# The grouped norm of the scan in four column strips, with its factor spread by one-row products

## What is computed

```
u = y.reshape(b, L, SSD_INNER) * jax.nn.silu(z.astype(f32))
ug = u.reshape(b, L, SSD_GROUPS, SSD_INNER // SSD_GROUPS)
ug = ug * lax.rsqrt(jnp.mean(ug * ug, axis=-1, keepdims=True) + EPS)
u = (ug.reshape(b, L, SSD_INNER) * norm_w.astype(f32)).astype(h.dtype)
y_ssd = u @ w_ssd_out
```

## Time and profile before

| | |
|---|---|
| median of 3 runs | 1366.25 us (1364.44 to 1367.7) |
| the profiled execution, its own time | 1368.92 us |
| its span in the profile | 1367.2 us |
| TensorE busy | 1214.0 us, 89% of the span |
| VectorE busy | 552.6 us, 40% |
| ScalarE busy | 389.2 us, 28% |
| GpSimd busy | 462.5 us, 34% |
| TensorE's share of the chain that ended last | 61% |
| mean granted clock of TensorE | 0.963 of full speed |

### The profile page before, as it was taken

How to read it: one execution, slowest core, us unless ns; L and a number is a source line. 1 busy time by engine, 2 the same in 40 slices (tenths; PEclk the granted TensorE clock), 3 DMA queues, 4 the chain that set the end, 5 groups by cost and what they waited for, 6 DMA issues and landing times.

```text
span 1367.2 us, 22226 instructions
## 1 busy us (share of the span) xinstructions
PE 1214.0 (89%) x8633; PEld 1038.6 (76%) x8633; DVE 552.6 (40%) x823; ACT 389.2 (28%) x572; POOL 462.5 (34%) x358
## 2 busy tenths in 40 slices
PE   4999999999998999989989999999996978877771
PEld 4999999999876976887687679999995645443440
DVE  5445532003654955585576563014443241021112
ACT  4122124343324433342343362222324101010112
POOL 5444432333533444263345354344220111111100
PEclk7999999999999999999999999999997999999996
DMA  6232222324203510540252123343639899999974
GB/s 151 64 91 77 77 62 62 83 76 126 70 17 102 139 47 1 159 108 20 73 152 63 31 87 89 83 126 103 226 122 383 322 396 401 403 398 383 393 254 148
DMA packets 185571, 210.75 MB, mean 154 GB/s; under 512 B 12166, under 2 KB 161798, under 8 KB 176754
## 3 DMA queue, kind: packets, MB, share of 16 engines
q1 hardware_dynamic: 176626, 193.41, 42.6%
q0 software_dynamic: 5040, 9.72, 2.8%
q10 hardware_dynamic: 3822, 6.39, 1.2%
HBM read 191.56 MB, written 26.57 MB: 160 GB/s over the span
## 4 chain that ended last, share of the span: by engine, by line
PE 61%; DVE 11%; DMA 9%; SPq 9%; issue 5%; ACT 4%; DVEq 1%; ACTq 0%; POOLq 0%
PE acc L627 37%; SPq L549 8%; DVE area L1202 4%; PE acc L890 4%; PE pTS L1010 3%; DMA area<-in_w_down 2%; PE pTS L739 2%; DMA area<-in_w_up 2%; PE acc L1040 2%; DMA ring<-in_w_in 2%; DMA ring<-in_w_up 2%; PE pTS L797 1%; PE pY L791 1%; PE pY L815 1%; DVE big L1264 1%
## 5 line engine op out<-in xcount | busy, mean ns | idle before, releaser
L627 PE MATMUL acc<-h_parts,ring_parts 128*128 128x328 f32 (+1 forms) x3840 | 546.9, 303 | 21.7 <-issue 7.0
L627 PEld LDWEIGHTS acc<-h_parts,ring_parts 128*128 128x128 f32 x3840 | 532.6, 190 | 38.1 <-issue 37.9
L1858 POOL TENSOR_TENSOR ring_parts<-ring,ring_parts 128x1024 fp32r<-128x1024 f32 x112 | 283.0, 2527 | 461.4 <-ACT ring_parts L1566 461.4
L1566 ACT ACTIVATE ring_parts<-ring 128x1024 fp32r<-128x1024 f32 x112 | 118.4, 1058 | 414.1 <-PE acc L627 366.9
L1010 PE MATMUL pTS<-area,big 128*64 128x256 f32 x672 | 109.1, 404 | 17.0 <-DMA area<-in_w_gate 7.2
L627 PE MATMUL acc<-u_parts,ring_parts 128*128 128x264 f32 (+1 forms) x640 | 109.4, 299 | 0.0
L1010 PEld LDWEIGHTS pTS<-area,big 128*64 128x64 f32 x672 | 66.5, 145 | 50.2 <-DMA area<-in_w_gate 10.8
L627 PEld LDWEIGHTS acc<-u_parts,ring_parts 128*128 128x128 f32 x640 | 96.4, 188 | 0.0
L1202 DVE SCALAR_TENSOR_TENSOR area<-area,xvec 128x616 f32<-128x616 f32 x72 | 90.1, 1252 | 10.5 <-DVE area L1200 0.6
L627 PE MATMUL acc<-area_parts,ring_parts 128*128 128x264 f32 (+1 forms) x512 | 91.1, 299 | 0.0
L627 PEld LDWEIGHTS acc<-area_parts,ring_parts 128*128 128x128 f32 x512 | 78.4, 188 | 0.0
(11 more groups left out here) (349 smaller groups left out, 1523.8 us busy)
## 6 DMA issues: line engine op xcount, KB each, us to landing
ring<-in_w_in SPq DMA_DIRECT2D x80, 512.0 KB, 3.9
area<-in_w_gate SPq DMA_DIRECT2D x21, 1024.0 KB, 17.6
area<-in_w_up SPq DMA_DIRECT2D x21, 1024.0 KB, 18.8
area<-in_w_down SPq DMA_DIRECT2D x21, 1024.0 KB, 23.9
area<-in_state_ssm SPq DMA_DIRECT2D x16, 512.0 KB, 6.8
out<-area SPq DMA_DIRECT2D x16, 512.0 KB, 6.7
ring<-in_w_ssd_out SPq DMA_DIRECT2D x16, 512.0 KB, 4.0
ring<-in_w_gate SPq DMA_DIRECT2D x7, 1024.0 KB, 24.0
```

What stands on the lines that cost most here:

```text
L627: m = nc.tensor.matmul(acc[a][:, h, 0:n], w[s][:, k, :], x[:, k, h * HALF:h * HALF + n], start=first and k == 0 and w is w_hi and x is hi, ...
L1566: a_.activation(w_hi[b % 2], w_raw[b % 2], ACT.Copy).then_inc(hi_done, 1)
L1858: gp.tensor_tensor(w_lo[b % 2], w_raw[b % 2], w_hi[b % 2].bitcast(F32), ALU.subtract).then_inc(lo_done, 1)
```

## The change

A constant `QT` = 148, a quarter of the tokens, is new.

1. The sums: for each of the four depth steps four products of 32 columns of ones by 148 tokens. Strip j of the array takes tokens 148 j onward and writes partitions 32 j to 32 j + 31 of `pT`. So each quarter's sum stands on 32 partitions, at the same columns.
2. The root and the reciprocal are one instruction each, on all 128 partitions and 148 columns.
3. TensorE then spreads the reciprocal: for each quarter a product of one row of ones (row 32 j) by one row of `rms`, into `pT` (quarters 0, 1) and `pS` (2, 3). The order is 0, 2, 1, 3, with a wait for the first two before the third, as quarters of one bank come from different rows of the array.
4. VectorE multiplies u by the factor from PSUM, in 8 instructions of 296 columns in place of 4 of 592.
5. TensorE: block 11 moves from the start of the next turn to before the jump, its first half ahead of the sums, its second half behind them, then the wait for `s_rm` and the spreading. So the loop's turn begins with block 2. Block 1 of the first group moves ahead of the loop, and the gate blocks after it begin with 2.
6. The wait for `s_rm` before the transposes becomes one for `s_un`; counts of semaphores follow.

```diff
             pe.wait_ge(s_dta, 7)
-            pe_block(pe, g_block(0, 0), 0, hT_hi, hT_lo)
+            for b in range(2):
+                pe_block(pe, g_block(0, b), b, hT_hi, hT_lo)
             with pe.Fori(0, GROUPS) as g:
-                for b in range(1, 7):
+                for b in range(2, 7):
                     pe_block(pe, g_block(g, b), b, hT_hi, hT_lo)
                 pe_block(pe, g_block(g, 7), 7, hT_hi, hT_lo, part=0)
                 pe.wait_ge(s_silu, g * 6 + 8)
-                pe.wait_ge(s_rm, g + 1)
+                pe.wait_ge(s_un, g + 1)
...
+                pe_block(pe, g_block(g, 11), 11, hT_hi, hT_lo, part=0)
                 pe.wait_ge(s_so, g + 1)
                 pe.wait_ge(s_sq, g + 1)
-                for h, pb in ((0, pT), (1, pS)):
-                    n = HALF if h == 0 else T - HALF
-                    for k in range(GK):
-                        m = nc.tensor.matmul(pb[:, 0:n], ones[:, :], sq[:, k, h * HALF:h * HALF + n],
+                for k in range(GK):
+                    for j in range(4):
+                        m = nc.tensor.matmul(pT[32 * j:32 * j + 32, 0:QT], ones[:, 0:32], sq[:, k, j * QT:(j + 1) * QT],
                                              start=k == 0, stop=k == GK - 1)
                 m.then_inc(p_gn, 1)
-
-            for n in range(1, 4):
+                pe_block(pe, g_block(g, 11), 11, hT_hi, hT_lo, part=1)
+                pe.wait_ge(s_rm, g * 2 + 2)
+                for j in (0, 2, 1, 3):
+                    if j == 1:
+                        pe.wait_ge(p_gn, g * 5 + 3)
+                    nc.tensor.matmul((pT, pS)[j // 2][:, j % 2 * QT:(j % 2 + 1) * QT], ones[32 * j:32 * j + 1, :],
+                                     rms[32 * j:32 * j + 1, :], start=True, stop=True).then_inc(p_gn, 1)
+
+            for n in range(2, 4):
...
-                dve.wait_ge(s_rm, g + 2)
+                dve.wait_ge(s_rm, g * 2 + 1)
                 link(v.reciprocal(rms, rms))
+                dve.sem_inc(s_rm, 1)
+                dve.wait_ge(p_gn, g * 5 + 5)
                 for k in range(GK):
                     u_k = uT[:, bass.ds(g * GK + k, 1), :].rearrange("p a b -> p (a b)")
-                    x = v.scalar_tensor_tensor(u_k, u_k, dg[:, k, 1:2], rms, ALU.mult, ALU.mult)
+                    for q, pb in ((0, pT), (1, pS)):
+                        u_q = u_k[:, q * 2 * QT:(q + 1) * 2 * QT]
+                        x = v.scalar_tensor_tensor(u_q, u_q, dg[:, k, 1:2], pb[:, 0:2 * QT], ALU.mult, ALU.mult)
...
-                act.wait_ge(p_gn, g + 1)
-                a_.activation(rms[:, 0:HALF], pT[:, 0:HALF], ACT.Sqrt, bias=eps[:, :], scale=1.0 / GW)
-                a_.activation(rms[:, HALF:T], pS[:, 0:T - HALF], ACT.Sqrt, bias=eps[:, :], scale=1.0 / GW).then_inc(s_rm, 1)
+                act.wait_ge(p_gn, g * 5 + 1)
+                a_.activation(rms, pT[:, 0:QT], ACT.Sqrt, bias=eps[:, :], scale=1.0 / GW).then_inc(s_rm, 1)
```

More of the change, by code:

```diff
@@ L24 @@
 HALF = TP // 2
+QT = T // 4
 HEADS, HD, NST, GROUPS = 32, 64, 128, 4
@@ L164, in build @@
         wts, o = carve(o, [2, 4 * P])
-        rms, _ = carve(o, [T])
+        rms, _ = carve(o, [QT])
         ytok, o = carve(o, [GW])
@@ L1066, in _ @@
             dve.sem_inc(s_y1, 1)
+            dve.sem_inc(s_un, 1)
             dve.sem_inc(s_cvd, 2)
@@ L1259, in _ @@
                 v.tensor_tensor(u_g, u_g, sz, ALU.mult).then_inc(s_uz, 1)
-                dve.wait_ge(s_rm, g + 2)
+                dve.wait_ge(s_rm, g * 2 + 1)
                 link(v.reciprocal(rms, rms))
+                dve.sem_inc(s_rm, 1)
+                dve.wait_ge(p_gn, g * 5 + 5)
                 for k in range(GK):
                     u_k = uT[:, bass.ds(g * GK + k, 1), :].rearrange("p a b -> p (a b)")
-                    x = v.scalar_tensor_tensor(u_k, u_k, dg[:, k, 1:2], rms, ALU.mult, ALU.mult)
+                    for q, pb in ((0, pT), (1, pS)):
+                        u_q = u_k[:, q * 2 * QT:(q + 1) * 2 * QT]
+                        x = v.scalar_tensor_tensor(u_q, u_q, dg[:, k, 1:2], pb[:, 0:2 * QT], ALU.mult, ALU.mult)
                 x.then_inc(s_un, 1)
-                dve.wait_ge(s_un, g + 1)
+                dve.wait_ge(s_un, g + 2)
                 assert link.count[0] == 25, link.count
@@ L1543, in _ @@
             act.sem_inc(so_out, 1)
-            act.sem_inc(s_rm, 1)
             act.sem_inc(f_out, 1)
@@ L1720, in _ @@
             for c in range(4):
-                act.wait_ge(s_un, c + 1)
+                act.wait_ge(s_un, c + 2)
                 a_.activation(uT_hi[:, 4 * c:4 * c + 4, :], uT[:, 4 * c:4 * c + 4, :], ACT.Copy).then_inc(u_hi, 1)
```

## The result

The changed kernel takes 1360.03 us (median of 8 runs, 1354.91 to 1362.12) beside 1366.97 us for the kernel before (8 runs). The ratio is 0.9935 with a 95% interval of 0.992 to 0.9951, so it is faster by 0.65%. The forecast was 1372.9 us, slower, with a range from 1367.0 to 1378.5. The profiled execution took 1362.0 us, its span is 1360.3.

What follows compares the result with a forecast made beforehand. TensorE's next work was taken as the bound, with the jump losing its cover and the clock falling: three turns at +2.4 us, less 0.55, gave +6.6 on the 1366.25 median, so 1372.9 us (1367.0 to 1378.5).

Steps and rivals of the forecast that it cites:

- the price of the jump: TensorE's taken branch back to the top of the group loop: 5.2 us per turn, with bounds 3.0 to 5.9.
- a jump under 4.3 us: Sign named in advance that the forecast is wrong: below this branch price a group turn is shorter than before.
- The jump is issued at 445.8: TensorE's group loop: branch issued once the last wait between the spreading products is past, with 0.3 us of work over it.
- ScalarE's chain does not move: Norm on ScalarE: weight block's DMA still ends at 441.19 and the root still starts at 443.56.
- Sums of 1 to 2 us: Norm's sums on TensorE in four strips: 1.0 us by width, 2 taken, where they took 4.22.
- TensorE done at 442.0: End of sums and both block halves in a group turn, before the norm's rows return; 444.0 with serial sums.
- The waits on the split and on the SiLU: TensorE's idle 1.32 us on GpSimd's weight split and 0.86 us on the last SiLU, both claimed to go.
- Restart at 451.25, transposes at 488.6: TensorE after the jump, then the next group's transposes with the clock loss included, 2.7 us later than 485.92.
- At the 215 ns of the short loop: Side case for the group loop's jump: VectorE's chain would be the bound, near 483.4, and the time 1358 us.
- (c): Faster rival: the jump costs 3.0 us, restart 449.05, clock as over the old gap; -4.4 us, 1361.9 us; chance 0.08.
- The clock falls at each restart: TensorE after each jump: granted clock drops to 1.2 GHz after idling, costing 1.7 us, with bounds 0 and 3.4.
- The last group brings 0.55 us: Last group, without a jump: one shorter root brings ScalarE's copies forward, -0.55 us (0 to -1).

Runs made afterwards that it cites:

- e1: Kernel before with 48 idle semaphore increments at the start of TensorE's program, so its loop touches 7 pages by count; ratio to before 0.9995.
- e5: Kernel before with 48 idle increments mostly hidden in TensorE's first loop, 8 ahead of each block, 7 pages; 1362.07 us, ratio to before 0.9948.
- e2: Changed kernel with 90 idle increments at the start of TensorE's program, 8 pages; 1383.81 us, ratio to before 1.0124.
- e6: Changed kernel with 90 idle increments in TensorE's first loop, 15 ahead of each block, 8 pages; 1379.98 us, ratio to before 1.0079.
- e7: Kernel before with only block 11 moved, in halves around the sums, wide norm kept, 7 pages; 1370.45 us, ratio to before 0.9998.
- e8: Kernel before with only the narrow norm, block 1 left behind the jump, e5's increments, 7 pages; 1383.87 us, ratio to before 1.0107.
- e9: Changed kernel with the strips' products about twice as wide (296 columns, last strip 148); 1358.61 us, ratio to before 0.994.
- e3: Changed kernel with 50 idle increments at the start of TensorE's program, still 7 pages by count; span 1364.7 us, one run only.
- e4: Changed kernel with ScalarE's root ahead of its split of the next weight block; 1352.8 us, ratio to before 0.989.
- e10: e5 with ScalarE's two roots ahead of its split of the next weight block, wide norm kept; 1358.3 us, ratio to before 0.9921.

## Why the prediction was wrong

**The step that failed** is the price of the jump: "The short loop at L706 pays 215 ns for the same instruction: the price belongs to this long body." The rows were read rightly, but the conclusion was carried too far: the price belongs to this body at this place in the program. The change itself moves the place, by putting block 1 ahead of the loop, an edit to which the prediction gave no cost. 5.2 us were in the sum for each turn; 0.21 was measured. e1 and e5 take the price away from the kernel before, and e2 and e6 give it to the kernel after. The prediction's own sign of being wrong, a jump under 4.3 us, is what came.

**Point by point.**
- The jump is issued at 445.8: it was 444.8. "ScalarE's chain does not move" was a second, smaller slip: the weight block landed at 440.07 and not at 441.19, though the sums started 3.1 us later, and the root with it at 442.44.
- Sums of 1 to 2 us: 1.21. TensorE done at 442.0: 438.03 + 3.90 = 441.93, in part by luck, as the sums took 0.8 us less than the 2 us in the sum, and the two halves of the block were together as much later. Root 0.4, reciprocal 1.0, spreading 0.3 to 0.6 a pair: 0.38, 1.08, and 1.14 for both pairs. The signal to TensorE, taken at 0.2 us from no row: 0.12 (443.93 to 444.05). TensorE idle before `s_rm` for 3 us: 2.12. VectorE's products 4.2: 3.55, and the convolutions start at 450.10. The waits on the split and on the SiLU are gone. This part of the drawing holds.
- Restart at 451.25, transposes at 488.6: 445.24 and 482.81. The 6 us are the 5.0 of the jump and the 1.0 of its issue.
- "At the 215 ns of the short loop" (behind rival (c)): this side case stood at 483.4 and 1358 us, within 2 us of what came. Its bound, VectorE's chain, was not reached: the transposes follow TensorE's own matmuls with no wait. The case was dismissed by the row of the jump, and with it the one that would have been right; (c) itself stopped at 3.0 us. And the 4.3 us at which (c) turns over hold only if the clock holds; with the sum's own 1.7 us of clock and 0.3 that come back it is 2.9. The Trainium skill's 108 ns (Advanced Engine Details and Errata, Control Flow Timing) is half of the measured 0.208 us, so nearer than the row, as long as the target is in the instruction memory.
- The clock falls at each restart and costs 1.7 us: it cost about 1.5 at all four. The size was right by luck, since the reason given did not occur. I argued from an idle time of 5 us; what stands ahead of the fall at 446 is an idle 2.12 us and one-row products, and the old 2.12 us had no fall behind it. Where a gap of 4.83 us did stand (e6), the 264 matmuls took 37.17 us, 1.3 more than at full clock, and 38.20 behind the 4.73 us of e2.
- The last group brings 0.55 us: gate block 2 starts 7.98 us after the sums, with half a block (2.9) ahead of them, where it was 11.48: 0.6 us. The fall of the clock then takes 1.5.
- The sum by measured terms: 3 x -3.4 - 0.6 + 1.5 = -9.3, of which 2.2 are lost behind the output projection.

**Was the change good for its own reason?** By the turns, at equal pages: 121.0 with neither half, 122.8 with the move, 127.3 with the narrow norm, 119.8 with both. Only both together help, by 1.2 us a turn; e7 and e8 each carry stretches at the low clock, so their size is rough. The larger part of the 3.4, 2.1 us, is the place of the code. With 8 pages the same edit is slower than the kernel before: by the turns, which leave out the late start, by 1.7 us (e6) and 1.2 us (e2), where 2.4 was forecast. There the sign of the forecast holds.

**What stays open.** Why the clock falls behind one restart and holds behind the next in the same kernel (e9) isn't settled, nor what sets the low stretches in the scan stage of e7 and in e6; they make some 1.5 us each and blur every comparison of totals under some 3 us. The page boundary was placed by one row; any shift from 45 to 73 instructions against the program's own start, where I used 59, would sort all kernels here alike. That the code's place sets the branch's price is shown by e1, e2, e3, e5 and e6; that the border lies between 7 and 8 pages rests on this count.

## What to carry to other kernels

Before a taken branch gets a price, ask whether its target is still in the instruction memory: look for instruction packets and for a second idle time a few instructions behind the jump, count the body in pages of 256, and find out how many it touches; an edit anywhere ahead of the loop can change that, and a few hidden instructions can put it right. Where engines wait for each other in a ring, put the short link that others wait for (the root) ahead of the one that waits for a DMA: that was worth 3 us a turn where the clock held, 2.5 to 2.8 over all three turns (e4, e10), more than the whole narrow norm. And test a gain against a version that has only its side effect (e1, e5), or the reason for it is not known.

## What the runs showed of the hardware

- A loop on TensorE jumps back in 0.21 us where its body touches 7 pages of 256 instructions by the count above, and in 4.4 to 5.9 us where it touches 8; some 9 more instruction packets come with each such jump. The Trainium skill (Advanced Engine Details and Errata, ISA Cache) gives 128 KB on TensorE, which is eight such pages; it also says "Only 2 cache lines!", and these runs disagree: seven pages stay. That one of the eight is taken by the page fetched ahead would explain it, but was only argued.
- The fetch also seems to delay other transfers: ScalarE's wait for the weight block beside it is 7.50 us in the kernel before, 7.09 and 7.15 at its other two jumps, and 5.8 to 6.1 in e1 and e5, whose code there is the same. In e2 and e6, where the fetch comes only after the block has landed, it is 5.8 to 6.0. This was read from the traces and not tested by itself.
- Eight one-row passes of 148 columns take 1.14 us (0.14 each), 32 passes in four strips of 32 columns 1.21 us. In e8, behind 8.55 us of idling and with the granted clock at 0.50, the same eight take 1.82 us. Reading PSUM, VectorE's product of 296 columns takes 3.55 / 8 = 0.44 us.
- An instruction that only counts up a semaphore costs some 0.09 us on an idle TensorE (48 of them 4.2 us). In e5, where 48 stand in a loop that runs four times, the first block starts 1.1 us later for the 8 ahead of it, and the others are mostly hidden.
